# One list of arrivals for the opening block, and places of their own for eight weight slots

## The reference, cut to what matters

```python
def first_block(x, c, ada_w, ada_b, pre1_w, ...):
    c_act = jax.nn.silu(c)
    mod = c_act @ ada_w[l] + ada_b[l]
    sh1, sc1, gt1, sh2, sc2, gt2 = [m[:, None, :] for m in jnp.split(mod, 6, axis=-1)]
    h = rms_norm(x, pre1_w[l]) * (1.0 + sc1) + sh1
    y = hybrid_mixer(h, w_in[l], ...)          # begins with h @ w_in
    ...

def second_block(x, mem, ...):
    for layer in range(2):
        ...
        mem_kv = (mem @ w_mem_kv[layer]).reshape(b, MEM_LEN, 2, N_MEM_HEADS, HEAD_DIM)
        mem_out = memory_attention(q_mem, mem_kv[:, :, 0], mem_kv[:, :, 1])
    ...
```

## Time and profile before

| what | value |
|---|---|
| median of 3 runs | 3115.06 us (3112.76 to 3116.66) |
| the profiled execution, its own time | 3120.65 us |
| its span in the profile | 3118.9 us |
| granted clock of TensorE, mean of the span | 0.949 |
| TensorE busy (matmul) | 2895.3 us |
| VectorE, ScalarE, GpSimd busy | 1600.3, 1065.8, 985.6 us |
| moved by transfers | 290.55 MB, mean 93 GB/s |
| moved in the first 100 us | 23.39 MB, mean 234 GB/s |

### The profile page before, as it was taken

The page is one execution under the profiler, slowest core; times in us unless marked ns, Lnnn a source line. Parts: engine busy times, 40 slices in busy tenths (PEclk is TensorE's granted clock), DMA queues, the critical chain, the costliest instruction groups (busy, mean ns, idle before and its releaser), DMA issues. The chain is left out here.

```text
span 3118.9 us, 34809 instructions
## 1 busy us (share of the span) xinstructions
PE 2895.3 (93%) x14150; PEld 2193.4 (70%) x14150; DVE 1600.3 (51%) x1726; ACT 1065.8 (34%) x1474; POOL 985.6 (32%) x537
## 2 busy tenths in 40 slices
PE   6999999999997989799999999899899998999887
PEld 5777777777775568577888788677566666777555
DVE  4263011316245453655555598632467673749557
ACT  3342212212216112433333345334433441347313
POOL 3232111213432121345555434531233331333102
PEclk8989999999998989899999999999999999999898
DMA  7111114562114244212222554412300002121201
GB/s 292 49 55 55 55 54 142 184 227 70 69 55 142 95 142 148 81 48 81 82 81 82 190 199 146 144 52 75 132 21 21 21 20 76 61 81 34 98 14 54
DMA packets 87601, 290.55 MB, mean 93 GB/s; under 512 B 8993, under 2 KB 13489, under 8 KB 86289
## 3 DMA queue, kind: packets, MB, share of 16 engines
q1 hardware_dynamic: 87442, 288.33, 27.5%
HBM read 223.70 MB, written 64.59 MB: 92 GB/s over the span
## 5 line engine op out<-in xcount | busy, mean ns | idle before, releaser
L282 POOL TENSOR_TENSOR w_lo_sb<-raw_w_sb,w_hi_sb 128x1024 fp32r<-128x1024 f32 x155 | 385.7, 2490 | 1263.2 <-ACT w_hi_sb L273 1263.1
L290 PE MATMUL ps<-h_hi_sb,w_hi_sb 128*128 128x512 f32 x720 | 301.5, 419 | 10.3 <-PEq L537 5.4
L290 PE MATMUL ps<-h_lo_sb,w_hi_sb 128*128 128x512 f32 x720 | 289.3, 402 | 0.0
L290 PE MATMUL ps<-h_hi_sb,w_lo_sb 128*128 128x512 f32 x720 | 251.6, 402 | 0.0
L273 ACT ACTIVATE w_hi_sb<-raw_w_sb 128x1024 fp32r<-128x1024 f32 x155 | 163.3, 1054 | 215.5 <-PE ps L290 165.3
L290 PE MATMUL ps<-z_lo,w_hi_sb 128*128 128x512 f32 x512 | 205.0, 400 | 0.0
L290 PE MATMUL ps<-merged_parts_hi_sb,w_hi_sb 128*128 128x512 f32 x472 | 191.4, 406 | 13.2 <-DVE merged_parts_lo_sb L2775 8.1
L290 PE MATMUL ps<-merged_parts_lo_sb,w_hi_sb 128*128 128x512 f32 x472 | 187.0, 396 | 0.0
L290 PEld LDWEIGHTS ps<-h_hi_sb,w_hi_sb 128*128 128x128 f32 x720 | 138.5, 192 | 56.2 <-issue 22.6
L290 PE MATMUL ps<-merged_parts_hi_sb,w_lo_sb 128*128 128x512 f32 x472 | 177.6, 398 | 0.0
L290 PE MATMUL ps<-z_hi,w_hi_sb 128*128 128x512 f32 x384 | 162.3, 423 | 14.2 <-PEq L912 5.9
(11 more groups left out here) (676 smaller groups left out, 6766.6 us busy)
## 6 DMA issues: line engine op xcount, KB each, us to landing
raw_w_sb<-in_w SPq DMA_DIRECT2D x237, 512.0 KB, 3.6
ada_late_sb<-in_ada SPq DMA_DIRECT2D x32, 512.0 KB, 3.7
inbox_sb<-gates_out SPq DMA_DIRECT2D x24, 512.0 KB, 4.0
ffn_hidden_out<-ffn_hidden_box_sb SPq DMA_DIRECT2D x22, 512.0 KB, 6.2
ffn_hidden_sb<-ffn_hidden_out SPq DMA_DIRECT2D x21, 512.0 KB, 6.3
ada_w<-in_ada SPq DMA_DIRECT2D x16, 512.0 KB, 9.0
gates_out<-outbox_sb SPq DMA_DIRECT2D x16, 512.0 KB, 2.6
inbox_sb<-sums_out SPq DMA_DIRECT2D x16, 512.0 KB, 5.0
```

The costliest lines, as they stand in the source:

```text
L282: nc.gpsimd.tensor_tensor(w_lo[:, n % RING].rearrange("p t m -> p (t m)"), raw_w[:, n % RAW], flat_hi, ALU.subtract).then_inc(w_split.sem, 1)
L290: mm = nc.tensor.matmul(o, wt, xs, start=start and part == 0 and xs is x_hi, stop=stop and part == 1, skip_group_check=again)
```

## The change: what it does

1. **One list.** The transfers of the constants, the memory, weight slots 0 to 9, the 16 modulation slots and the four quarters of `x` stand in one list, `fetched`, in the order in which SP issues them. From their sizes and an assumed 0.39 MB/us the list gives a planned arrival (`lands`) for each, and the planned times of all parts follow from these arrivals instead of from fixed steps (`S`, `X`, `K`, `split_at`).
2. **Places.** Weight slots 0 to 7 go to eight places of their own (`kv_raw`), over the high half of `H`, each with a semaphore of its own. They wait for no earlier slot. Slots 8 and on use `raw_w` as before; since its two semaphores are then raised by 64 less each, the first memset of each layer on VectorE raises one of them by 64. The first high part of `normed` waits until eight slots have been split.
3. **The memory** has a place of its own, and its two parts lie over tiles 4 to 7 of the low half of `H`. The waits for the last K step move from tiles 0 and 1 to tiles 4 and 5.
4. **Orders.** The roundings of slots 4 to 11 on ScalarE are no longer tied to the taking of keys; `first_slots` places all of them by `split_at`. Stores of keys and values, statistics and `heads_in` get planned times from the list.

```diff
-            S = lambda n: 12.0 + 2.2 * n
-            X = lambda i: 4.0 + 8.0 * i
-            K = lambda n: 15.0 + 3.2 * n
-            N0 = S(ADA_EARLY) + 2.0
+            kv_raw = sb_over("kv_weights_in", [P, 8, SLOT * P], F32, h_lo_at - 4 * DT * T)
+            kv_full = [sem(f"kv_weights_in{n}") for n in range(8)]
+            MB_US = 0.39
+            fetched = [("vec", 0), ("cst", 0), ("mem", 0), ("w", 0), ("w", 1), ("x", 0), ("ada", 0), ("w", 2), ("ada", 1),
+                       ("w", 3), ("x", 1), ("ada", 2), ("w", 4), ("ada", 3), ("w", 5), ("ada", 4), ("x", 2), ("w", 6),
+                       ("ada", 5), ("w", 7), ("ada", 6), ("x", 3), ("ada", 7), ("ada", 8), ("ada", 9), ("w", 8),
+                       ("ada", 10), ("w", 9), ("ada", 11), ("ada", 12), ("ada", 13), ("ada", 14), ("ada", 15)]
+            megabytes = {"vec": 0.15, "cst": 0.6, "w": 0.524, "mem": 1.05, "ada": 0.524, "x": 1.05}
+            lands, now = {}, 0.0
+            for what, n in fetched:
+                now += megabytes[what] / MB_US
+                lands[(what, n)] = now + 2.5
...
+            K, split_at, at = [], [], lands[("mem", 0)] + 5.5
+            for n in range(8):
+                ready = max(lands[("w", n)] + 1.5, split_at[-1] + 2.6 if n else 0.0)
+                split_at.append(max(ready, K[n - RING] + 4.8) if n >= RING else ready)
+                at = max(at, split_at[n] + 2.6)
+                K.append(at)
+                at += 4.2
+            K.append(at)
...
+            FOLDED = S[-1] + 3.0
+            H0 = FOLDED + 4.0
...
                 def on_sp(sp):
-                    yield -10.0
-                    sp.dma_start(vec[:], a["vec"]).then_inc(loaded.sem, 16)
-                    sp.dma_start(cst[:], a["cst"]).then_inc(loaded.sem, 16)
-                    for n in range(ADA_EARLY):
-                        yield S(n - ADA_RING) + 1.0
-                        if n >= ADA_RING:
-                            sp.wait_ge(ada_done.sem, n - ADA_RING + 1)
-                        sp.dma_start(ada_w[:, n % ADA_RING].rearrange("p k m -> p (k m)"), a["ada"][n]
-                                     ).then_inc(ada_full[n % ADA_RING].sem, 16)
+                    for what, n in fetched:
+                        yield lands[(what, n)] - 12.0
...
+                        if what == "w" and n < 8:
+                            sp.dma_start(kv_raw[:, n], a["w"][n]).then_inc(kv_full[n].sem, 16)
+                        if what == "w" and n >= 8:
+                            sp.dma_start(raw_w[:, n % RAW], a["w"][n]).then_inc(w_full[n % RAW].sem, 16)
+                        if what == "ada":
+                            if n >= ADA_RING:
+                                sp.wait_ge(ada_done.sem, n - ADA_RING + 1)
+                            sp.dma_start(ada_w[:, n % ADA_RING].rearrange("p k m -> p (k m)"), a["ada"][n]
+                                         ).then_inc(ada_full[n % ADA_RING].sem, 16)
...
             def first_slots():
                 def on_sp(sp):
-                    for n in range(RING + 8 + RAW):
-                        yield -3.0 + 0.1 * n if n < RAW else split_at(n - RAW) + 2.6
-                        if n >= RAW:
-                            sp.wait_ge(w_split.sem, n - RAW + 1)
+                    for n in range(8 + RAW, RING + 8 + RAW):
+                        yield split_at[n - RAW] + 2.6
+                        sp.wait_ge(w_split.sem, n - RAW + 1)
                         sp.dma_start(raw_w[:, n % RAW], a["w"][n]).then_inc(w_full[n % RAW].sem, 16)
 
                 def on_act(act, link):
-                    for n in range(RING):
-                        yield split_at(n) - 1.4
-                        round_slot(act, None, n, 0)
+                    for n in range(RING + 8):
+                        yield split_at[n] - 1.4
+                        if n >= RING:
+                            act.wait_ge(kv_t.sem, n - RING + 1)
+                        if n >= 8:
+                            round_slot(act, None, n, 0)
+                            continue
+                        act.wait_ge(kv_full[n].sem, 16)
+                        nc.scalar.activation(w_hi[:, n % RING].rearrange("p t m -> p (t m)"), kv_raw[:, n], ACT.Copy
+                                             ).then_inc(w_rounded.sem, 1)
...
-                        yield X(i) + 7.0 + 0.8 * (t % 4)
+                        yield X(i) + 0.6 + 1.0 * (t % 4)
...
-                            if n == 2:
+                            if n == 6:
                                 dve.wait_ge(kv_t.sem, 8)
...
+                        if n == 0:
+                            act.wait_ge(w_split.sem, 8)
                         act.wait_ge(scaled_s.sem, n + 1)
...
-                        if n == 1:
+                        if n == 5:
                             pool.wait_ge(kv_t.sem, 8)
...
-            memT = sb_over("mem_in", [P, DT, MEM], F32, h_lo_at)
-            MT = (sb_over("mem_parts_hi", [P, DT, MEM], F32R, h_lo_at + 8 * T),
-                  sb_over("mem_parts_lo", [P, DT, MEM], F32R, h_lo_at + 16 * T))
+            memT = sb_in(scope, "mem_in", [P, DT, MEM])
+            MT = (sb_over("mem_parts_hi", [P, DT, MEM], F32R, h_lo_at + 16 * T),
+                  sb_over("mem_parts_lo", [P, DT, MEM], F32R, h_lo_at + 24 * T))
...
-                        yield K(4 * layer + 4) + 3.0
+                        yield max(K[4 * layer + 4] + 2.0, lands[("ada", ADA_EARLY - 1)] - 6.0)
                         sp.wait_ge(one_s.sem, layer + 1)
...
-                            yield K(n + 1) + 0.2
+                            yield K[n] + 3.6
                             act.wait_ge(kv_t.sem, n + 1)
...
-                            round_slot(act, None, n + RING, 0)
-                        for part in range(2):
-                            n = 4 * layer + 2 + part
-                            yield K(n + 1) + 0.3
-                            act.wait_ge(kv_t.sem, n + 1)
-                            round_slot(act, None, n + RING, 0)
...
-                        nc.vector.memset(km[layer][64:65], 1.0)
+                        nc.vector.memset(km[layer][64:65], 1.0).then_inc(w_full[layer % RAW].sem, 16 * 8 // RAW)
...
-                at = X(2 * h + 1) + 12.0
+                at = X(2 * h + 1) + 6.5
...
-            heads_in = dense(N0 + 6.0, 5, 8, from_h, ["act", "act", "dve", "dve", "act"], emit, PAIRS,
+            heads_in = dense(H0, 5, 8, from_h, ["act", "act", "dve", "dve", "act"], emit, PAIRS,
```

More of the change, by code:

```diff
@@ new lines, in build @@
+            megabytes = {"vec": 0.15, "cst": 0.6, "w": 0.524, "mem": 1.05, "ada": 0.524, "x": 1.05}
[3 more added lines that the diff above has]
+                lands[(what, n)] = now + 2.5
+            S, at = [], 0.0
+            for n in range(ADA_EARLY):
+                at = max(lands[("ada", n)] + 0.3, at + 1.0)
+                S.append(at)
+            X = lambda i: lands[("x", i)]
+            K, split_at, at = [], [], lands[("mem", 0)] + 5.5
@@ new lines, in build @@
+            for n in range(8):
[5 more added lines that the diff above has]
+            K.append(at)
+            for n in range(8, 12):
+                ready = lands[("w", n)] + 1.5 if n < 8 + RAW else split_at[n - RAW] + 8.5
+                split_at.append(max(ready, split_at[-1] + 2.6, K[n - RING] + 4.8))
@@ L993, in modulation @@
+            FOLDED = S[-1] + 3.0
+            H0 = FOLDED + 4.0
             def modulation():
                 def on_sp(sp):
[L995 to L1003 removed]
+                    for what, n in fetched:
+                        yield lands[(what, n)] - 12.0
+                        if what == "vec":
+                            sp.dma_start(vec[:], a["vec"]).then_inc(loaded.sem, 16)
+                        if what == "cst":
+                            sp.dma_start(cst[:], a["cst"]).then_inc(loaded.sem, 16)
+                        if what == "mem":
+                            sp.dma_start(memT[:], a["mem"]).then_inc(mem_s.sem, 16)
+                        if what == "w" and n < 8:
[7 more added lines that the diff above has]
+                                         ).then_inc(ada_full[n % ADA_RING].sem, 16)
+                        if what == "x":
+                            where = slice(4 * (n % 2), 4 * (n % 2) + 4), tokens(n // 2)
+                            sp.dma_start(x0[:, where[0], where[1]], a["x"][:, where[0], where[1]]).then_inc(x_s[n].sem, 16)
@@ L1005, in on_pe @@
                 def on_pe(pe):
                     for n in range(ADA_EARLY):
-                        yield S(n)
+                        yield S[n]
                         if n == 0:
@@ L1062, in squares @@
                 quarters = [(2 * h + k, h, t) for h in range(2) for k in range(2) for t in range(4 * k, 4 * k + 4)]
-                def on_sp(sp):
-                    for i in range(4):
-                        yield X(i)
-                        where = slice(4 * (i % 2), 4 * (i % 2) + 4), tokens(i // 2)
```

(15 more changed lines are left out.)

27 lines of the change are left out of this document (15 added, 12 removed).

## The result

The changed kernel took 3093.35 us (median of 4 runs, 3090.05 to 3098.42) beside 3114.93 for the kernel before (4 runs): a ratio of 0.9939, 95% interval [0.9925, 0.9953], or 19 us (15 to 23). The forecast was 3105.2 with a range of 3097.5 to 3112.0. The profiled execution was the slowest of the four, 3098.42 (span 3096.6), 22.2 less than the one before. The ratios of this document leave out two executions, both of the kernel with a busy later start, which took 3630 and 3633 us at a mean granted clock of 0.736.

The account below looks back on a forecast made before the run. Two raw-weight places and queue order were taken to bound the opening; `heads_in` would start at 69.8 instead of 79.69. Profiled 3120.65 minus 9.9 gives 3110.8, less 5.6 above the median: 3105.2 us, range 3097.5 to 3112.

Parts of the forecast that it names:

- What bounds the kernel: Opening before TensorE's dense work: two places for raw weights, with the queue's order, delay `heads_in` to 79.69 us.
- Arrivals, K(0): Start of opening: memory arrives at 7.9 us, first key/value step ends near 20.8, gaining only 0.4.
- TensorE from there: TensorE after the first key/value step, nearly gapless: modulation slot 9 ends at 52.9 us, slot 15 at 59.4.
- Queue's tail decides: End of the transfer queue: stores and weight slots 10, 11 set `heads_in`'s start; slot 11 visible at 65.4 us.
- The pair of stores at 3.2: Transfer queue's tail: each layer's key and value stores, 0.8 MB, take 3.2 us; plain rate would give 2.0.
- Behind slot 11: Opening's end: rounding to 66.5, GpSimd low part to 68.9, stalled input low part to 69.7; `heads_in` at 69.8 us.
- The sum: Whole kernel: profiled 3120.65 us minus 9.9 gives 3110.8; less 5.6 above the median, 3105.2.
- Two executions differ by up to 4 us: Whole kernel: spread between executions up to 4 us; 0.2%, 6.2 us, about what can be told from no change.
- Rival 1: Opening: the transfer queue's tail sets the start; 3105.2 us, own range 3101 to 3109, chance 0.52.
- Rival 2: Opening: stores overlap reads, slot 11 split by 60; `heads_in` at 63.6, 16 us gained, 3099 us, chance 0.12.
- Rival 3: Opening: TensorE's chain runs later, delaying modulation slot 15 and weight slots 10, 11; 3109 to 3112 us, chance 0.26.
- Rivals 4 and 5: Opening: TensorE stays at low clock, 3123 us, chance 0.05; or waits still hold the queue, 3115 us, chance 0.05.

Follow-up runs that it names:

- busy later start: Changed kernel with 24 unneeded TensorE matmuls added before `heads_in`; ratio 0.9992 to the kernel before.
- the repeat: Changed kernel, nothing edited, timed again: 3097.08 us (6 runs) beside 3111.38 (22 runs) for the kernel before, ratio 0.9956.
- engines' orders alone: Changed kernel, but SP in the order of the kernel before and weight slots through two raw places; ratio 1.0023 to the kernel before.
- stores last: Changed kernel with both layers' key and value stores behind the transfers of slots 10 and 11; ratio 0.9945 to the kernel before.
- splits later: Changed kernel with stores behind slots 10 and 11, whose rounding and GpSimd low parts also move later, among the input tiles; ratio 0.9949 to the kernel before.

## Why the prediction was right or wrong

**What bounds the kernel.** Right that a change to the opening pays only by an earlier start of the dense work, and that this is passed on one to one: the table shows it, as far as the intervals can tell. Half wrong that the two raw places, together with the order of the queue, bound the opening: with both places kept, the order gave 11.7 of 13.8 us; without the new order, places of their own gave nothing that shows in the time.

**Arrivals, K(0).** Memory at 7.85 (forecast 7.9), K(0) through by 20.03, and by 20.93 in the repeat (20.8). The gain there is small, as said.

**"TensorE from there": too long by 4.4 at S(9).** S(9) ended at 48.5, not 52.9. K(0) gave 0.8. K(1) was priced from a row in which half ran at the low clock, 4.3, and took 3.06 (20.61 to 23.67); with S(0) 0.64 instead of 0.9 that is 1.5. Statistic 0 took 0.95 instead of 1.87, a price also read at a low clock. The remaining 1.2 is spread over fifteen K and S steps of about 0.1 or less each. In the repeat S(9) ended 3.2 early, with nothing gained at K(0): the prices were too high by 3.6 and 3.4 us in the two profiles. I took the price of each step from the one row that I had and put "K(1) wholly at full clock" only in the rival's own range; nearly all my errors lay on that side. Behind S(9) it went the other way: VectorE's last two adds of squares took 5.64 us (two such took 1.49 at 41.65 in the same profile, with nothing on GpSimd) beside rest(8) and rest(9), TensorE stood 2.39 for them and then ran at the low clock, so S(15) ended at 58.9, close to my 59.4 by two errors that cancel. It cost little here, since the tail decided: in the repeat S(15) ended 1.0 later still and `heads_in` began no later.

**"Queue's tail decides": right, in both profiles of the changed kernel. The pair of stores at 3.2: wrong.** From S(9)'s end to slot 11 visible I had 12.5 and it took 13.3. The second pair of stores took 61.78 - 58.33 - 1.31 = 2.1, not 3.2, and 1.96 in the repeat: this is the plain rate that I had beside it as a bound. The 3.2 was itself one execution's: the second profile of the kernel before gives 63.40 - 58.66 - 2x1.31 = 2.1 for the same pair. The first part was slower: slot 10 was visible 9.8 behind S(9), not 8.05, though its own pair of stores stands in it. Together +0.8. So slot 11 came at 61.78, not 65.4: -4.4 + 0.8 = -3.6. In the repeat the shares are -3.2 and -0.5, and their sum is the same: the stretch behind S(9) isn't of fixed length, as I had it. An estimate by the Trainium skill, DMA: Bandwidth & Descriptors, "why a DMA increments its semaphore by 16", had also given 2.0 for a pair. The 2.1 agrees with it and with the plain rate alike, so it doesn't show which holds.

**Behind slot 11:** rounding, rest and stalled low part took 4.0 to the end of the low part (4.3 forecast), and `heads_in` followed at 65.92 instead of 69.8. The stall of the low part behind GpSimd was as forecast in kind (1.40 instead of 0.75). One I had not seen: the adding of the bias, 16 columns from two SBUF tensors, took 2.16 instead of 0.17, because it met rest(10): by these rows the tail held up the start more by this, 2.0, than by the stalled low part, 0.65 (my estimate from the durations beside their plain ones). The Trainium skill, SBUF — State Buffer, "SBUF: two separate sides", has the rule: a VectorE operation with two SBUF inputs and a GpSimd operation shut each other out for a whole instruction. Four places here agree: 2.16, 2.37 and 2.26 for 0.17, 2.88 for 0.75. In the repeat the bias, which began later beside rest(10), took 1.21.

**The sum.** 3.9 of the 11.9 us that were missing are the start of `heads_in`. The other 8.0 lie outside the opening, and the repeat doesn't have them: the 3115.06 that I subtracted from lies 3.7 above the kernel before's median beside the repeat (3111.38), and the first median after lies 3.7 below the repeat's 3097.08; together 7.4. By the repeat's ratio of 0.9956 the changed kernel stands at 3101.4 for a kernel before at 3115.06. That is 3.8 below the forecast and inside the range. Three terms failed as put. "TensorE from there" had S(9) end at 52.9 by low-clock prices, and it ended at 48.5. The pair of stores stood at 3.2, read from one execution, and took 2.1. And "Two executions differ by up to 4 us", which set the range, was read off the three executions of the median (3112.76 to 3116.66), though the profiled one beside them stood at 3120.65.

How far do executions differ? The 62 executions of the kernel before that ran beside the experiments went from 3104.2 to 3120.5, with a median near 3111.2, while the four behind the first ratio began at 3112.8. Four drawn at random from the 62 have a median of 3114.93 or more in about one draw of 80. So chance is a possible but strained account of the first median before; whether something else, such as another chip, made these executions slower, no run shows.

**Rivals.** Rival 1 is the one that happened, with a start 3.9 earlier than its own; the 3093.35 lies below its range of 3101 to 3109, the 3101.4 by the repeat's ratio at its edge. Rival 2 (tail hidden, 3099) has nearly the measured time for another reason: nothing was hidden, rest(11) was the last to arrive. Rival 3's fear came in the wrong place, with the chain late behind S(9) and not before it. Rivals 4 and 5 did not happen, though engines' orders alone is a slower case that I had not thought of: +7 us, from engines' orders that fit another order of arrivals.

**Open.** Why TensorE was granted the low clock from statistic 1 on in some executions wasn't tried. The length of the pause ahead of it doesn't tell: after 2.39 us (the changed kernel) and 2.09 (its repeat) the statistic took 1.87 and 1.51, after 2.13 (stores last) and 2.10 (splits later) it took 1.05, at full clock. So how much of the 2.5 us of stores last is that of the stores stays open too. Nor was a version tried that takes the rests of slots 10 and 11 off GpSimd altogether, which by my estimate might gain the 2.9 us by which splits later began earlier.

## What to carry to other kernels

A queue's order and the orders of the engines behind it are one schedule: judge and change them together, since here neither half alone brought any of what both gained. Look at what stands behind a wait in an engine's list: both halves lost by a tiny inverse root queued behind a rounding whose slot came late. The last things in a queue set when its consumers start, so put stores behind the loads that something waits for, and look at what a GpSimd pass does to every two-input VectorE operation on the critical chain, however small. Moving such a pass is no gain unless it lands where nothing waits. Take a step's price from rows at both clocks and from more than one execution, and hold a gain of less than 1% against the spread of many executions, not of three.

## What the runs showed of the hardware

- **Low clock wanders.** The time from the third taking of q to the end, the same work in all kernels, lay between 2995.5 and 3008.3 us in the twelve profiles whose granted clock reached 1.00 (all but that of the busy later start). The first profile of before had 286.8 us at the low clock from the third taking of q on, the second 266.3, stores last 256.1. Over 62 executions of the kernel before, the mean granted clock and the time go together (correlation -0.76): a median of 3106.8 at 0.955, 3111.4 at 0.953, 3119.4 at 0.949. Two profiles of one kernel differ by 20.5 us of low clock, so nothing here ties a difference between kernels to the change.
- **Two VectorE operations on 16 and 8 columns took 2.37 and 2.26 us** where 0.17 each is plain, one behind each of two GpSimd operations that ran back to back: what such a stall costs goes by what is left of GpSimd's operation (4.64 for the two), not by the length of VectorE's. In the repeat of the changed kernel the same 16 columns began 1.18 before the end of rest(10) and took 1.21.
- **A pair of stores of 0.8 MB between two reads of the same queue** added 2.1 and 2.0 us in the two profiles of the changed kernel, and 3.2 and 2.1 in the two of the kernel before. What made the one 1.1 longer, no run shows.
